# Seven block products and additions in place of eight: the two long merges of a hybrid encoder step

## What is computed

```
gt = jax.nn.sigmoid(g_branch.reshape(B, T, N_BRANCH, D_MODEL))     # g_branch = columns of h @ w_in
merged = (gt[:, :, 0] * (o_a @ w_branch_a) + gt[:, :, 1] * (o_g @ w_branch_g)
          + gt[:, :, 2] * (o_m @ w_branch_m))
x1 = x + merged @ w_out
y = x1 + hmoe(x1, ...)
```

## Time and profile before

| | |
|---|---|
| Median of 3 runs | 1650.2 us (1649.73 to 1651.55) |
| The profiled execution's own time | 1652.53 us |
| Its span, first to last instruction | 1650.8 us |
| Granted TensorE clock, mean over the span | 0.966 |
| TensorE matmul busy | 1516.8 us, 92% |
| VectorE / ScalarE / GpSimd busy | 33% / 18% / 7% |

### The profile page before, as it was taken

How to read it: one execution, slowest core, us unless ns; L and a number is a source line. 1 busy time by engine, 2 the same in 40 slices (tenths; PEclk the granted TensorE clock), 3 DMA queues, 4 the chain that set the end, 5 groups by cost and what they waited for, 6 DMA issues and landing times.

```text
span 1650.8 us, 16912 instructions
## 1 busy us (share of the span) xinstructions
PE 1516.8 (92%) x6626; PEld 842.6 (51%) x6626; DVE 540.3 (33%) x1513; ACT 294.9 (18%) x682; POOL 112.8 (7%) x172
## 2 busy tenths in 40 slices
PE   5999999998899999987999999999999998997772
PEld 3554555445455544455555544576555465554441
DVE  2205498205500031544000144334465154111013
ACT  3214210213200010124201011234400021110100
POOL 6000000112000000001000100000000001111000
PEclk9999999899899999999999999999999997999996
DMA  7331120111332416325021431022023736999995
GB/s 207 106 103 39 39 52 25 52 51 52 115 108 58 140 52 212 93 70 211 33 70 51 150 102 60 18 72 77 26 61 117 322 145 214 420 420 420 421 396 214
DMA packets 127579, 230.88 MB, mean 140 GB/s; under 512 B 12241, under 2 KB 90065, under 8 KB 112529
## 3 DMA queue, kind: packets, MB, share of 16 engines
q1 hardware_dynamic: 114672, 183.03, 31.1%
q0 software_dynamic: 12832, 46.84, 7.9%
HBM read 214.21 MB, written 21.92 MB: 143 GB/s over the span
## 4 chain that ended last, share of the span: by engine, by line
PE 81%; DMA 12%; DVE 4%; ACT 2%; issue 1%; SPq 0%; POOL 0%; POOLq 0%; DVEq 0%; ACTq 0%
PE ps L707 18%; PE ps L726 7%; PE ps L638 7%; PE ps L628 7%; DMA bulk<-in_w_exp_up 5%; PE ps L1159 4%; PE ps L657 3%; PE ps L677 3%; PE ps L587 3%; PE ps L1226 3%; DMA arena<-in_w_exp_up 2%; DMA bulk<-in_w_exp_down 2%; PE ps L629 2%; PE ps L639 2%; PE ps L727 2%; PE ps L1249 2%
## 5 line engine op out<-in xcount | busy, mean ns | idle before, releaser
L707 PE MATMUL ps<-bulk 128*128 128x512 f32 x688 | 303.0, 596 | 2.3 <-issue 2.3
L707 PEld LDWEIGHTS ps<-bulk 128*128 128x128 f32 x688 | 129.3, 191 | 155.9 <-issue 155.9
L726 PE MATMUL ps<-bulk 128*128 128x512 f32 x256 | 135.1, 609 | 0.0
L638 PE MATMUL ps<-arena,bulk 128*128 128x512 f32 x256 | 131.1, 594 | 1.8 <-DVE arena L1795 1.8
L628 PE MATMUL ps<-bulk 128*128 128x512 f32 x256 | 131.1, 594 | 0.0
L1226 PE MATMUL ps<-bulk,arena 128*64 128x256 f32 x704 | 88.4, 386 | 17.2 <-DMA bulk<-in_w_exp_gate 8.3
L1226 PEld LDWEIGHTS ps<-bulk,arena 128*64 128x64 f32 x704 | 59.2, 139 | 46.5 <-issue 27.5
L727 PEld LDWEIGHTS ps<-bulk 128*128 128x128 f32 x256 | 48.6, 190 | 61.2 <-issue 61.2
L639 PEld LDWEIGHTS ps<-arena,bulk 128*128 128x128 f32 x256 | 48.6, 190 | 61.2 <-issue 61.2
L629 PEld LDWEIGHTS ps<-bulk 128*128 128x128 f32 x256 | 48.6, 190 | 61.2 <-issue 61.2
L1159 PE MATMUL ps<-bulk 128*128 128x512 f32 x160 | 71.8, 605 | 2.1 <-issue 2.1
(11 more groups left out here) (395 smaller groups left out, 2025.2 us busy)
## 6 DMA issues: line engine op xcount, KB each, us to landing
bulk<-in_w_in SPq DMA_DIRECT2D x48, 512.0 KB, 4.0
bulk<-in_w_exp_gate SPq DMA_DIRECT2D x22, 1024.0 KB, 29.1
bulk<-in_w_exp_up SPq DMA_DIRECT2D x22, 1024.0 KB, 27.7
bulk<-in_w_exp_down SPq DMA_DIRECT2D x22, 1024.0 KB, 29.0
bulk<-in_w_in SPq DMA_DIRECT2D x7, 2048.0 KB, 10.7
arena<-in_w_exp_down SPq DMA_DIRECT2D x10, 1024.0 KB, 27.7
arena<-in_w_exp_gate SPq DMA_DIRECT2D x10, 1024.0 KB, 28.8
arena<-in_w_exp_up SPq DMA_DIRECT2D x10, 1024.0 KB, 28.4
```

The source lines that it names most:

```text
L638: mm(ps[4 * q][:, 0:TP], tw[2 * q + 1][:, k, :], src[:, k, 0:TP], start=k == 0, stop=k == KD - 1)
L707: last = mm(ps[4 + n % 2][:, :], lhs[:, k, tok:tok + P], ring[f % 2][:, k, :], start=k == 0, stop=k == KD - 1)
L726: mm(ps[b][:, 0:TP], tw[s][:, k, :], hT[:, k, 0:TP], start=k == 0, stop=k == KD - 1)
```

## The change

In merges 0 and 1 the two column blocks i and i + 4, the two halves of the 1024 input rows and the two halves of the 640 tokens form a 2 x 2 by 2 x 2 block product. It is done with seven block products (each 4 matmuls of 128 x 320) instead of eight, after Strassen in Winograd's form. The first gate pair of each merge is still done directly, with two 320-token halves; so each merge has 7 such rounds (r = 0..6 for m = 0, r = 7..13 for m = 1): branch pair i = 0, then gate and branch pair for i = 1, 2, 3.

For it VectorE forms four sums of token blocks (`token_sums`, once per source and merge, 128 x 1280 each) and four sums of weight blocks per round (`weight_sums`, 128 x 512 each), and puts the products together with seven additions of 128 x 320 per round (`four_quarters`). ScalarE copies the first product out (`first_out`) and runs the sigmoids of later pairs from SBUF in place. Four banks belong to gates, four to branches. The sums lie where the memory cache's first tiles were loaded early, so GpSimd loads these after merge 0; the SyncE loop of merge 1 is unrolled, and the order of the fills is gate, gate, branch, branch.

```
@@ TensorE
+            def seven_products(r, u, i, q, x, ts, ss):
+                a, b, c, d = (ps[n][:, 0:TH] for n in banks[q])
+                top, low = tw[q], tw[q + 2]
+                pe.wait_ge(tw_in[q], 16 * (u + i))
+                quarter(a, top[:, 0:KH, :], x[:, 0:KH, 0:TH])[-1].then_inc(p_full, 1)
+                pe.wait_ge(sum_ok, SUM + r + 1)
+                pe.wait_ge(tw_in[q + 2], 16 * (u + i))
+                quarter(b, ss[1], ts[1])[-1].then_inc(p_full, 1)
+                quarter(c, ss[2], ts[2])[-1].then_inc(p_full, 1)
+                quarter(d, ss[0], ts[0])[-1].then_inc(p_full, 1)
+                pe.wait_ge(m1_ok, M1 + r + 1)
+                quarter(a, top[:, KH:KD, :], x[:, KH:KD, 0:TH])[-1].then_inc(p_full, 1)
+                pe.wait_ge(kept, KEPT + 6 * r + 1)
+                made = quarter(c, low[:, KH:KD, :], ts[3])
+                made[0].then_inc(t_full[q], 1)
...
+                pe.wait_ge(kept, KEPT + 6 * r + 3)
+                made = quarter(d, ss[3], x[:, KH:KD, TH:T])
+                made[0].then_inc(t_full[q + 2], 1)
...
+                for q in range(2):
+                    pe.wait_ge(m_prod[q], 4 * m + 1)
+                    pe.wait_ge(tw_in[2 * q], 16 * u)
+                    if q and before_branch is not None:
+                        before_branch()
+                    elif q:
+                        pe.wait_ge(*ready)
...
+                pe.wait_ge(*ready)
+                for i in range(KH):
+                    if i:
+                        for q in range(2):
+                            pe.wait_ge(sg_ok[q], 4 * m + i)
+                        seven_products(7 * m + 2 * i - 1, u, i, 0, hT, gate_t[m], gate_s[m])
                     for q in range(2):
-                        block_step(pe.snap(i + 1), q)
+                        pe.wait_ge(m_prod[q], 4 * m + 1 + i)
+                    seven_products(7 * m + 2 * i, u, i, 1, src, branch_t[m], branch_s[m])
@@ ScalarE
+                def first_out(r, q):
+                    act.wait_ge(p_full, PF + 7 * r + 1)
+                    if r:
+                        act.wait_ge(kept, KEPT + 6 * (r - 1) + 4)
+                    go(first, ps[banks[q][0]][:, 0:TH], ACT.Copy).then_inc(m1_ok, 1)
@@ VectorE
+            def token_sums(x, ts):
+                lo, hi = x[:, 0:KH, :], x[:, KH:KD, :]
+                link(v.tensor_tensor(ts[0], lo[:, :, TH:T], lo[:, :, 0:TH], ALU.subtract))
+                link(v.tensor_tensor(ts[1], hi[:, :, TH:T], ts[0], ALU.subtract))
+                v.tensor_tensor(ts[2], hi[:, :, TH:T], lo[:, :, TH:T], ALU.subtract)
+                v.tensor_tensor(ts[3], hi[:, :, 0:TH], ts[1], ALU.subtract)
+            def four_quarters(r, q, top, low, between):
+                dve.wait_ge(m1_ok, M1 + r + 1)
+                dve.wait_ge(p_full, PF + 7 * r + 2)
+                link(v.tensor_tensor(u2, b, first, ALU.add))
+                dve.wait_ge(p_full, PF + 7 * r + 3)
+                v.tensor_tensor(u3, c, u2, ALU.add).then_inc(kept, 1)
+                dve.wait_ge(p_full, PF + 7 * r + 4)
+                dve.wait_ge(kept, KEPT + 6 * r + 1)
+                v.tensor_tensor(low[:, TH:T], d, u3, ALU.add).then_inc(kept, 1)
+                v.tensor_tensor(u4, d, u2, ALU.add).then_inc(kept, 1)
+                between()
+                dve.wait_ge(p_full, PF + 7 * r + 5)
+                v.tensor_tensor(top[:, 0:TH], a, first, ALU.add).then_inc(kept, 1)
+                dve.wait_ge(p_full, PF + 7 * r + 6)
+                v.tensor_tensor(low[:, 0:TH], c, u3, ALU.add).then_inc(kept, 1)
+                dve.wait_ge(p_full, PF + 7 * r + 7)
+                dve.wait_ge(kept, KEPT + 6 * r + 3)
+                v.tensor_tensor(top[:, TH:T], d, u4, ALU.add).then_inc(kept, 1)
...
+            dve.wait_ge(ke_ok, KE + NT)
+            token_sums(hT, gate_t[0])
             gla_gated(NT - 1)
...
+            dve.wait_ge(og_ok, NT)
+            token_sums(goT, branch_t[0])
+            dve.wait_ge(early_out, 48)
+            weight_sums(U_MERGE[0], 0, 1, branch_s[0])
             merge(U_MERGE[0], 0)
...
+            dve.wait_ge(osT_ok, OSTK + 2)
+            token_sums(qmT, branch_t[1])
+            weight_sums(U_MERGE[1], 0, 1, branch_s[1])
+            token_sums(hT, gate_t[1])
             merge(U_MERGE[1], 1)
@@ GpSimd
-            pool.wait_ge(og_ok, NT)
             pool.wait_ge(early_out, 48)
+            for q in range(2):
+                pool.wait_ge(m_prod[q], 4 + 1)
```

More of the change, by code:

```diff
@@ L501, in _ @@
                 wide_fill(f)
-            merge_job(1, U_MERGE[1])
+            for i in range(4):
+                merge_fill(1, U_MERGE[1], i)
             for f in range(8, 11):
@@ L627, in block_step @@
                     for k in range(KD):
-                        mm(ps[4 * q + 1][:, 0:TP], tw[2 * q][:, k, :], hT[:, k, 0:TP], start=k == 0, stop=k == KD - 1)
-                        last = mm(ps[4 * q + 3][:, 0:TS], tw[2 * q][:, k, :], hT[:, k, TP:T],
-                                  start=k == 0, stop=k == KD - 1)
+                        for h in range(2):
+                            last = mm(ps[banks[0][2 * q + h]][:, 0:TH], tw[2 * q][:, k, :], hT[:, k, halves[h]],
+                                      start=k == 0, stop=k == KD - 1)
@@ L631, in block_step @@
                     last.then_inc(t_full[2 * q], 1)
[L632 to L640, removed]
@@ L1361, in gates @@
             def gates(u, m):
[L1363 to L1368, removed]
+                def first_out(r, q):
[3 more added lines that the diff above has]
+                    go(first, ps[banks[q][0]][:, 0:TH], ACT.Copy).then_inc(m1_ok, 1)
+                for q in range(2):
+                    act.wait_ge(m_prod[q], 4 * m + 1)
+                    act.wait_ge(t_full[2 * q], u + 1)
+                    for h in range(2):
+                        last = go(sg2[:, q, halves[h]], ps[banks[0][2 * q + h]][:, 0:TH], ACT.Sigmoid)
+                    last.then_inc(sg_ok[q], 1)
+                first_out(7 * m, 1)
+                for i in range(1, KH):
+                    r = 7 * m + 2 * i - 1
+                    first_out(r, 0)
+                    act.wait_ge(kept, KEPT + 6 * r + 5)
+                    go(sg2[:, 1, :], sg2[:, 1, :], ACT.Sigmoid).then_inc(sg_ok[1], 1)
+                    act.wait_ge(kept, KEPT + 6 * r + 6)
+                    go(sg2[:, 0, :], sg2[:, 0, :], ACT.Sigmoid).then_inc(sg_ok[0], 1)
+                    first_out(r + 1, 1)
             def gate_exp(n):
@@ new lines, in weight_sums @@
+            def weight_sums(u, i, q, ss):
+                for n in (q, q + 2):
+                    dve.wait_ge(tw_in[n], 16 * (u + i))
+                top, low = tw[q], tw[q + 2]
+                link(v.tensor_tensor(ss[0], low[:, 0:KH, :], low[:, KH:KD, :], ALU.add))
+                link(v.tensor_tensor(ss[1], ss[0], top[:, 0:KH, :], ALU.subtract))
+                v.tensor_tensor(ss[2], top[:, 0:KH, :], low[:, 0:KH, :], ALU.subtract)
+                v.tensor_tensor(ss[3], top[:, KH:KD, :], ss[1], ALU.subtract).then_inc(sum_ok, 1)
@@ new lines, in merge @@
+            def merge(u, m):
+                for i in range(KH):
+                    if i:
+                        four_quarters(7 * m + 2 * i - 1, 0, sg2[:, 0, :], sg2[:, 1, :], lambda: weight_sums(u, i, 1, branch_s[m]))
+                    r = 7 * m + 2 * i
+                    part = [prod2[:, q, :] if m else merged[:, i + KH * q, :] for q in range(2)]
+                    four_quarters(r, 1, part[0], part[1], lambda: weight_sums(u, i + 1, 0, gate_s[m]) if i + 1 < KH else None)
+                    for q in range(2):
+                        dve.wait_ge(sg_ok[q], 4 * m + i + 1)
+                    dve.wait_ge(kept, KEPT + 6 * r + 6)
+                    for q in range(2):
+                        v.tensor_tensor(part[q], part[q], sg2[:, q, :], ALU.mult).then_inc(m_prod[q], 1)
+                    if m:
+                        for q in range(2):
+                            dve.wait_ge(m_prod[q], 4 * m + 2 + i)
+                            sum_ = merged[:, i + KH * q, :]
+                            v.tensor_tensor(sum_, sum_, part[q], ALU.add).then_inc(merged_ok, 1)
```

71 lines of the change are left out of this document (33 added, 38 removed).

## The result

The changed kernel takes 1620.1 us in the median of 4 runs (1618.79 to 1623.53), the kernel before 1650.31 (4 runs). The ratio is 0.9819, 95% interval 0.9804 to 0.9835: 30.2 us or 1.8% faster. Forecast were 1624.3 us, range 1619 to 1631.

What follows compares the result with a forecast made beforehand. The prediction took columns streamed through TensorE to bound the merges. Columns 30.3, plus start of merge 0 1.5, less ends 2.5 and clock 3.4, save 25.9 us: median 1650.2 to 1624.3 us, range 1619 to 1631.

Steps and rivals of the forecast that it cites:

- What bounds the kernel: Both merges are bound by columns streamed through TensorE, 81% of the chain; VectorE, ScalarE and DMA have room.
- the case that I gave the best chance: Clock falls at both merge ends, rounds as priced: 1622 to 1628 us, chance 0.42.
- the first rival: The clock holds at one or both merge ends: 1619 to 1623 us, chance 0.30.
- The price of a column: TensorE in the merges: 0.541 us per 320-wide matmul, rounds 15.14 instead of 17.31 us, 30.3 us saved in all.
- Inside a round: VectorE's and ScalarE's added work in each merge round costs nothing; the weight sums lead by 4.6 us.
- Start of merge 0: A gate block fills TensorE's 1.75 us of idle time, a wait up to 0.3 remains: 1.5 us gained.
- Start of merge 1: Token and weight sums are hidden behind two gate blocks, with almost 10 us to spare.
- The ends: After each merge the next projections wait for both products, 2.40 us idle; costs 2.5 us for both merges.
- The clock: After both merge ends the granted clock falls to 0.50 for 3.4 us, costing 2 x 1.7 = 3.4 us.
- The gap of 2.61 us: An idle gap elsewhere in the old trace that left the clock at 1.00, so a fall is no certainty.
- The slower rival: Second block product waits 2 us or more every round and the clock falls each time: 1676 us, chance 0.03.
- Swallowed later: Transfers in a later stage, up to 12% DMA on the chain, eat the gain: 1640 to 1650 us, chance 0.05.

Runs made afterwards that it cites:

- e1_halves: The kernel before with every 512 + 128 pair of widths in the two merges made 320 + 320, no seven products: 1649.3 us, ratio 0.9991.
- e3_late_sums: The changed kernel with the next round's weight sums formed after the seventh addition of a round instead of the fourth: 1634.0 us, ratio 0.9902 to the kernel before.
- e4_more_sums: The changed kernel with the first weight sum of each round formed five times, in the same place: 1624.4 us, ratio 0.9837 to the kernel before.
- e5_late_long: The changed kernel with weight sums after the seventh addition and the first sum formed three times: 1668.1 us, ratio 1.0101 to the kernel before.
- e6_only_merge1: The kernel before with the seven products in merge 1 alone, merge 0 left as it was: 1638.9 us, ratio 0.9933.
- e8_changed_again: The changed kernel, unaltered, measured again beside the kernel before on one chip: 1621.6 us, ratio 0.9830.
- e7_long_end: The changed kernel with three more VectorE additions ahead of the last two multiplications of each merge: 1624.4 us, ratio 0.9850 to the kernel before.

## Why the prediction held, and where it was off

What bounds the kernel: right. The columns left out came out of the time nearly one for one, and VectorE's five-fold work in the merges did not show.

Which case came true: 1620.1 us is not the case that I gave the best chance (falls at both ends, 1622 to 1628 us, 0.42) but the first rival (the clock holds at one or both ends, 1619 to 1623 us, 0.30). The two profiles of the changed kernel have none and one fall.

The price of a column: right in kind, 0.4% high. 320-wide instructions are 0.269 us apart, I had 0.2705 from the mixed block; a round is 15.07 us against 15.14, a saving of 2.24 instead of 2.16, over 14 rounds 31.3 instead of 30.3. The direct gate pairs also gained a little by equal widths, 0.08 us by e1_halves. The estimate by the Trainium skill, "TensorE: Matmul & The Clock Gate", section Back-to-back issue gap, is 0.2717 us per instruction; the trace has 0.2692.

Inside a round: right. No wait is left in either merge beyond the first round's. The lead of the weight sums was put at 4.6 us and is 4.9. e3_late_sums and e4_more_sums show that this lead, and not VectorE's share, is what the change hangs on. A wait costs more than the idle time that the records show: 1.08 and 2.53 us idle cost 1.35 and 2.81.

Start of merge 0: right. I gave 1.75 less 0.3, it was 1.75 less about 0.2. With 2.9 us more of sums (e4_more_sums) the wait there grew by 2.9, as a place with no slack must.

Start of merge 1: right, no wait.

The ends: right. I had 2.40 us of idle time at the end of merge 0, it was 2.32; the two ends cost 2.3 us where I had 2.5.

The clock: this is the term that was mis-sized. I took a fall at both ends, 3.4 us, from the end of the third merge. In the first profile it fell at neither. There the forecast and the profiled spans part by 6.6 us (25.9 forecast, 32.5 measured): 3.4 for the clock, 1.3 for the inside of the merges (33.1 where I had 31.8), 0.2 for the ends and 1.7 for stages around the merges, which I had put at nothing. At the third merge's end the clock fell again in that profile, behind its own gap of 2.06 us:

```profile
1241.00:1244.40 3.40, 3.40 (x5) 1.35 (x4) 0.00 (x0) 0.00 (x0) 0.00 (x0) 0.50 0.82 211
```

But one row of a kind is no rule: over the eleven profiles on record the clock fell at the third merge's end in 6, and held in the other 5. The gap of 2.61 us that I named against it was no better a witness: in 9 of the eleven profiles the clock fell within 1.6 us behind that gap, and the kernel before happened to be one of the two where it held. And the earlier trace rows, cited for the clock behind the old ends, begin 10 us after the end. The windows right behind the two old ends do show it:

```profile
943.00:948.00 5.00, 3.90 (x11) 1.82 (x10) 1.71 (x3) 0.00 (x0) 3.46 (x5) 1.00 0.37 118
588.00:593.00 5.00, 3.78 (x10) 1.82 (x10) 0.89 (x2) 0.00 (x0) 0.00 (x0) 1.00 0.01 3
```

Over all profiles that have the end of 2.32 us (the changed kernel twice, e3, e4 and e5 with two ends each, e6 with one) the clock fell behind 6 of 11. By that rate two ends cost 1.9 us on average, not 3.4. With 31.3 for the columns and 1.9 for the clock the sum is 28.4 us, 1621.8; the measured gains are 30.2 and 28.4. So of the 4.2 us between 1624.3 and 1620.1 the clock's average accounts for 1.5 and the columns for 1.0; the remaining 1.7 is how these four runs fell, and e8_changed_again does not have it.

The slower rival's mechanism is real (e5_late_long, 1668 us; I had put 1676 for a fall every time). It did not come about because the sums have their lead. The Trainium skill, "TensorE: Matmul & The Clock Gate", section A second HAM failure mode: psum-queue depth-cycling, says that brief idling between groups while cycling PSUM banks lets the clock oscillate. Here, where the idling is a wait for VectorE's sums, that is so with gaps of 2.5 us (7 of 12) and not with gaps of 1.08 us (none of 12). Swallowed later: no; the stages behind merge 1 are 1.3 us shorter than before.

## What to carry to other kernels

Where TensorE streams without a gap, leave columns out: seven products for eight came back as 12.9% of a round (12.5 for the columns, the rest for the equal widths), since VectorE's eleven sums and additions per round, with up to four steps more behind a branch round, fit beside it. Form the operands of the next round well ahead of the point where they are wanted, here 4.9 us; the same instructions a few places later lost 14 to 16 us. When results move from PSUM through SBUF, ask again what the next stage really waits for: it needed a drained bank, not the finished product, and the old wait cost 5.1 us. And take the cost of a wait from the distance between starts, not from the idle time between records.

## What was not expected

A gap in TensorE's work does not decide alone whether the clock falls. Behind waits of equal length, with the same work on both sides in the same kernel, the granted clock fell to 0.50 for 3.4 us in 7 of 12 cases at 2.53 us; over several kernels it did in 6 of 11 at 2.32 us, in 2 of 2 at 3.90 us and in none of 12 at 1.08 us. What decides it is not shown. The half clock need not begin with the work either: in e5_late_long TensorE resumed at 504.74 and the clock fell at 506.1, and in e7_long_end it fell 0.6 us ahead of the work.

```profile
504.70:506.10 1.40, 1.36 (x5) 1.04 (x6) 0.00 (x0) 0.00 (x0) 0.00 (x0) 1.00 0.00 0
506.10:509.50 3.40, 3.40 (x8) 2.09 (x8) 0.49 (x1) 0.00 (x0) 0.00 (x0) 0.50 0.00 0
```

Such falls go with the spread of equal runs: of the ten of e6_only_merge1 the shortest (1630.1 us) has the highest mean clock, 0.972, and the two above 1642.5 have 0.961 and 0.963.
